# Feed-forward starts on unnormalised rows, and the next layer's modulation dealt out over more places

## What is computed

```python
def trunk_layer(l, x, cond, ctx):
    mod = (silu(cond) @ w_mod[l] + b_mod[l]).reshape(cond.shape[0], 6, D_MODEL)[:, :, None, :]
    h = rmsnorm(x, g_norm1[l]) * (1.0 + mod[:, 1]) + mod[:, 0]
    out, ctx_tensors = token_mixer(l, h, ctx)
    x = x + mod[:, 2] * out
    h = rmsnorm(x, g_norm2[l]) * (1.0 + mod[:, 4]) + mod[:, 3]
    x = x + mod[:, 5] * swiglu(h, w_ffn_in[l], w_ffn_out[l])
    return x, ctx_tensors

def swiglu(h, w_in, w_out):
    gte, up = jnp.split(h @ w_in, 2, axis=-1)
    return (jax.nn.silu(gte) * up) @ w_out
```

## Time and profile before

| | us |
|---|---|
| median of 3 runs | 3496.08 (3495.28 to 3497.89) |
| the profiled execution | 3492.04 |
| its span, first to last instruction | 3490.3 |
| PE busy, PE weight load busy | 3296.3, 3038.3 |
| DVE, ACT, POOL busy | 1967.6, 1114.6, 64.8 |
| mean granted TensorE clock | 0.977 of full |

### The profile page before, as it was taken

One profiled execution on the slowest core, in us unless ns is written; L12 is line 12 of the kernel. 1 busy time (PEld: TensorE's weight loads), 2 busy tenths in 40 slices (PEclk: granted clock), 3 DMA queues, 4 the chain that ended last, 5 costly groups with the idle time before them and its releaser, 6 DMA issues.

```text
span 3490.3 us, 54266 instructions
## 1 busy us (share of the span) xinstructions
PE 3296.3 (94%) x20704; PEld 3038.3 (87%) x20704; DVE 1967.6 (56%) x3034; ACT 1114.6 (32%) x1789; POOL 64.8 (2%) x48
## 2 busy tenths in 40 slices
PE   6899999999998999899999988999999987999999
PEld 3777688999996776899999956899999887999999
DVE  4233357757366665585763745686663788633333
ACT  2244432111134555321111434331111486311111
POOL 0211000000000000000000000000000000000000
PEclk8999999999999999999999999999999999999999
DMA  5111125444221110253532200153532221222222
GB/s 189 55 53 40 39 73 169 140 149 139 77 80 43 44 42 17 61 169 114 175 111 72 70 26 18 55 172 112 173 116 69 76 60 48 67 72 73 77 72 78
DMA packets 443966, 304.23 MB, mean 87 GB/s; under 512 B 12483, under 2 KB 422726, under 8 KB 442822
## 3 DMA queue, kind: packets, MB, share of 16 engines
q1 hardware_dynamic: 433508, 293.75, 27.0%
q10 hardware_dynamic: 10338, 8.88, 0.8%
HBM read 298.49 MB, written 4.10 MB: 87 GB/s over the span
## 4 chain that ended last, share of the span: by engine, by line
PE 85%; DVE 8%; ACT 3%; DVEq 2%; issue 2%; DMA 1%; ACTq 0%; SPq 0%
PE psB L319 30%; PE psA L319 29%; PE psD L319 7%; PE psC L382 3%; PE psA L363 3%; PE psC L335 2%; PE psB L363 2%; PE psC L374 2%; DVE work L2313 1%; PE psD L865 1%; DVE h_lo L2320 1%; DVE act_lo L2320 1%; PE psA L924 1%; DVE work L2627 1%; DMA tables<-in_w_mod 1%
## 5 line engine op out<-in xcount | busy, mean ns | idle before, releaser
L1621 ACT ACTIVATE w_hi<-raw 128x1024 fp32r<-128x1024 f32 (+1 forms) x315 | 325.9, 1036 | 1117.9 <-PE psB L319 758.4
L2215 DVE TENSOR_TENSOR w_lo<-raw,w_hi 128x1024 fp32r<-128x1024 f32 (+1 forms) x315 | 375.2, 1192 | 289.5 <-ACT w_hi L1621 289.1
L319 PE MATMUL psA<-act_hi,w_hi 128*128 128x320 f32 x1600 | 370.5, 313 | 20.4 <-DVE w_lo L2215 15.4
L319 PE MATMUL psB<-act_hi,w_hi 128*128 128x320 f32 x1600 | 369.3, 312 | 10.7 <-DVE w_lo L2215 10.7
L319 PE MATMUL psB<-act_hi,w_lo 128*128 128x320 f32 x1600 | 371.7, 314 | 0.0
L319 PE MATMUL psA<-act_hi,w_lo 128*128 128x320 f32 x1600 | 370.4, 313 | 0.0
L319 PE MATMUL psB<-act_lo,w_hi 128*128 128x320 f32 x1600 | 367.9, 311 | 0.0
L319 PE MATMUL psA<-act_lo,w_hi 128*128 128x320 f32 x1600 | 366.9, 311 | 0.0
L2245 DVE SCALAR_TENSOR_TENSOR work<-work,silu_c 128x1024 f32<-128x1024 f32 x252 | 312.6, 1282 | 11.6
L319 PEld LDWEIGHTS psA<-act_hi,w_hi 128*128 128x128 f32 x1600 | 272.4, 191 | 23.5 <-issue 16.4
L319 PEld LDWEIGHTS psB<-act_hi,w_hi 128*128 128x128 f32 x1600 | 274.8, 191 | 11.4 <-issue 11.4
(11 more groups left out here) (364 smaller groups left out, 5435.5 us busy)
## 6 DMA issues: line engine op xcount, KB each, us to landing
raw<-in_w_ffn_in SPq DMA_DIRECT2D x176, 512.0 KB, 3.8
work<-in_w_mod SPq DMA_DIRECT2D x144, 512.0 KB, 6.0
raw<-in_w_ffn_out SPq DMA_DIRECT2D x64, 512.0 KB, 4.0
raw<-in_w_ffn_out SPq DMA_DIRECT2D x32, 384.0 KB, 3.3
raw<-in_diff_w_in SPq DMA_DIRECT2D x24, 512.0 KB, 3.8
work<-in_w_mod SPq DMA_DIRECT2D x8, 1024.0 KB, 7.2
raw<-in_w_mod SPq DMA_DIRECT2D x16, 512.0 KB, 4.0
tables<-in_w_mod SPq DMA_DIRECT2D x16, 512.0 KB, 4.2
```

The costliest lines, as they stand in the source:

```text
L319: last = nc.tensor.matmul(out[:, b, 0:half], w[slot][:, kt * cols + c0:kt * cols + c0 + P], r[:, o:o + half], start=(kt == 0 and p == 0), ...
L1621: nc.scalar.activation(w_hi[s][:, 0:n], raw[s][:, 0:n], ACT.Copy).then_inc(hi_done, 1)
L2215: nc.vector.tensor_tensor(w_lo[s_][:, 0:n], raw[s_][:, 0:n], w_hi[s_][:, 0:n].bitcast(F32), ALU.subtract).then_inc(split_done, 1)
```

## The change

- **Feed-forward starts** (layers 0 to 3): four panels on unnormalised rows instead of two, that is tiles 0 and 1 with gate and up; tile 2 is the first on normalised rows. DVE rescales panel 1 and splits panel 3 inside the loop of `norm`, and rescales panels 2 and 3 behind it.
- **Layer 1's attention start**: three panels instead of two (query, key, value of head 0). The sums and rotations of head 0 are hung between matmuls of these panels, and four eighths of head 1's query panel go ahead of head 0's scores.
- **Modulation**: units are dealt out by a list of shares over hidden tiles and output turns; `mod_turn` stands at the start of the second place after the one that completes a kind. Kind 5 of layer 0 is dealt out with them as the first kind of its list (7 kinds, 56 units), and `late_wide` and `late_turn` go. Layer 0: 2 2 2 2 3 3 in `in0`, 2 in each turn of `out0`, 3 in each tile of `in1`, 2 in each turn of `out1`, 2 in the first tile of `in2`. Layers 1 and 2: 2 in each tile of `in0` and each turn of `out0`, 3 in each tile of `in1`, 1 in each turn of `out1`. SP issues units four ahead. DVE's loops over output turns are written out in layers 0 to 2.
- **First normalisation**: DVE multiplies x by `first_rms` as soon as that is there; gain and shift then go in two ACT instructions for each tile, in place, ACT copies the tile to hi, and DVE subtracts once for each tile.
- `gains_of` of the next layer stands ahead of the last output projection instead of ahead of chunk 2.

```diff
-FIRST_PANELS = [0, 2, 2, 2, 4, 2, 2, 2]
+MLEAD = 4
+FIRST_PANELS = [0, 4, 3, 4, 4, 4, 2, 4]
...
+        shares = ([2, 2, 2, 2, 3, 3] + [2] * 4 + [3] * 8 + [2] * 4 + [2]) if layer == 0 else [2] * 6 + [2] * 4 + [3] * 8 + [1] * 4
...
                 for g, (place, turn) in enumerate(turns):
+                    turn(place[2])
+                    if g == 2:
+                        mod_units(plan, range(MLEAD))
+                    if g > 2:
+                        mod_units(plan, plan.share(turns[g - 1][0]), MLEAD)
...
-                first_panels(2 * layer + 1, [(psA, 0, ph.number(0, 0)), (psB, 1, ph.number(0, 1))])
-                if layer == 0:
-                    late_wide()
+                first_panels(2 * layer + 1, [(psum[j], j, ph.number(i, j)) for i in range(2) for j in range(2)])
...
-                    first_panels(2, [(psD, 2, phases["diff"].first + 1), (psA, 0, phases["diff"].first + 2)])
-                    ssq(h0)
-                    gv(h0, 0, 2)
-                    acts.wait(pe, "rsq", h0)
-                    rotq(h0)
-                    gv(h0, 2, 4)
-                    ssk(h0)
-                    gv(h0, 4, 6)
+                    first_panels(2, [(psD, 2, first + 1), (psA, 0, first + 2), (psB, 1, first + 3)],
+                                 {(1, 5): lambda: ssq(h0), (2, 1): lambda: rotq(h0), (2, 5): lambda: ssk(h0)})
+                    gq(h1, 0, 2)
                     acts.wait(pe, "rsk", h0)
                     rotk(h0)
-                    gv(h0, 6, 8)
+                    gq(h1, 2, 4)
                     kturn(h0)
...
+                            nc.scalar.activation(source[:, o], source[:, o], ACT.Identity, bias=bias,
+                                                 scale=gains[:, cond * KT + kt:cond * KT + kt + 1])
+                    if n == 0:
+                        act.drain()
+                        last = nc.scalar.activation(hi[:, kt * T:(kt + 1) * T], source[:, kt * T:(kt + 1) * T], ACT.Copy)
...
+            dve.wait_ge(rstd_done, 1)
+            for kt in range(KT):
+                nc.vector.tensor_tensor(first_scaled[:, kt * T:(kt + 1) * T], x[:, kt * T:(kt + 1) * T], first_rms,
+                                        ALU.mult).then_inc(scaled_done, 1)
...
                 norm(n, {1: lambda: rescale(n, 0, psA, ph.number(0, 0), gate_silu),
-                         3: lambda: low_part(f"in{layer}.0", 1, 0)})
-                rescale(n, 1, psB, ph.number(0, 1), prod)
...
+                         3: lambda: low_part(f"in{layer}.0", 1, 0),
+                         5: lambda: rescale(n, 1, psB, ph.number(0, 1), prod),
+                         7: lambda: low_part(f"in{layer}.0", 1, 1)})
...
+                early_product(0, prod, gate_silu)
+                rescale(n, 2, psA, ph.number(1, 0), gate_silu2)
+                low_part(f"in{layer}.0", 2, 0)
+                rescale(n, 3, psB, ph.number(1, 1), prod2)
+                early_hidden(0, prod)
+                low_part(f"in{layer}.0", 2, 1)
+                early_product(1, prod2, gate_silu2)
+                early_hidden(1, prod2)
```

More of the change, by code:

```diff
@@ L121, in number, with __init__, share, plan_modulation @@
         return turn * self.n + (self.first + j + 1)
+class Modulation:
+    def __init__(self, layer, kinds, shares, first_unit, first_kind):
+        self.layer, self.kinds, self.first_unit, self.first_kind = layer, kinds, first_unit, first_kind
+        self.places = [(phase, ch, i) for ch, size in enumerate(FFN_CHUNKS)
+                       for phase, n in (("in", size), ("out", KT // 2)) for i in range(2 if (phase, ch) == ("in", 0) else 0, n)]
+        self.units, self.turns, self.sums = {}, {}, {}
+        at, done = 0, []
+        for p, (place, share) in enumerate(zip(self.places, shares)):
+            self.units[place] = range(at, at + share)
+            if at // KT < (at + share) // KT:
+                done.append(p)
+            at += share
+        assert at == len(kinds) * KT and len(done) == len(kinds)
+        for k, p in enumerate(done):
+            self.turns[self.places[p + 2]] = self.sums[self.places[p + 2]] = k
+            assert k + 2 >= len(kinds) or sum(shares[:p + 3]) <= (k + 2) * KT
+    def share(self, place):
+        return self.units.get(place, range(0))
+def plan_modulation():
+    plans, unit, kind = [], 0, 0
+    for layer in range(DEPTH - 1):
+        kinds = ([(0, 5)] if layer == 0 else []) + [(layer + 1, k) for k in range(6)]
+        shares = ([2, 2, 2, 2, 3, 3] + [2] * 4 + [3] * 8 + [2] * 4 + [2]) if layer == 0 else [2] * 6 + [2] * 4 + [3] * 8 + [1] * 4
+        plans.append(Modulation(layer, kinds, shares, unit, kind))
+        unit, kind = unit + len(kinds) * KT, kind + len(kinds)
+    return plans
 def plan_panels():
@@ L633, in turn, with panels @@
                                      source(g, j)).then_inc(raw_in[s], 16)
-                if units:
-                    turn(0)
-                    for g in range(ph.turns):
-                        if g + 1 < ph.turns:
-                            turn(g + 1)
-                        if behind_first and g == 0:
-                            behind_first()
-                        for u in range(TILE_UNITS):
-                            mod_unit(*units, g * TILE_UNITS + u)
-                    return
+                return turn
+            def panels(name, source):
+                ph, turn = phases[name], panel_turn(name, source)
                 peeled = 1 if ph.first == 0 else 0
@@ L2257, in mod_sums, with place_sums @@
                 last.then_inc(mod_summed, 1)
+                if layer == plan.layer:
+                    dve.drain()
+                    for cond in range(2):
+                        nc.vector.tensor_tensor(m_[:, :, cond], m_[:, :, cond],
+                                                bmod[:, layer * 48 + kind * KT:layer * 48 + (kind + 1) * KT], ALU.add)
+                    dve.drain()
+            def place_sums(plan, place):
+                if plan and place in plan.sums:
+                    mod_sums(plan, plan.sums[place])
             def mod_bias(layer):
                 m = mods[layer % 2][:, :].rearrange("p (k c) -> p k c", c=2)
-                dve.wait_ge(mod_summed, 6 * layer + 1)
+                dve.wait_ge(mod_summed, modulation[layer - 1].first_kind + len(modulation[layer - 1].kinds) + 1)
                 for cond in range(2):
@@ L2528, in _ @@
                     first = phases["diff"].first
-                    norm(2, {1: lambda: rescale(2, 0, psD, first + 1, dq_t[0])})
-                    rescale(2, 1, psA, first + 2, dk_t[0][:, 0:T])
                     h0 = Head(0, 0)
-                    for step in (q_normed, q_roped, k_normed, k_roped):
-                        step(h0)
-                    low(Head(0, 1), 0)
+                    norm(2, {1: lambda: rescale(2, 0, psD, first + 1, dq_t[0]), 3: lambda: low(Head(0, 1), 0),
+                             4: lambda: rescale(2, 1, psA, first + 2, dk_t[0][:, 0:T]), 5: lambda: q_normed(h0),
+                             6: lambda: q_roped(h0), 8: lambda: k_normed(h0)})
+                    rescale(2, 2, psB, first + 3, dvt)
+                    k_roped(h0)
                     low(Head(0, 1), 1)
```

275 lines of the change are left out of this document (128 added, 147 removed).

## The result

| | before | after |
|---|---|---|
| median of the timed executions, us | 3496.98 (3495.28 to 3498.16, 4) | 3440.08 (3439.37 to 3445.85, 4) |
| the profiled execution | 3492.04 | 3440.55 |
| its span | 3490.3 | 3438.8 |
| mean granted clock | 0.977 | 0.980 |

The ratio of after to before is 0.9842, 95% interval 0.9828 to 0.9855: 57 us faster by the medians, 51.5 by the two profiles. Brackets hold the lowest and highest time and, in the table, the number of executions. The forecast was 60.6 us and 3435.4.

What follows compares the result with a forecast made beforehand. PE, busy 94% of the span, was taken as the bound. Savings of 20.9 + 21.9 + 9.8 + 8.0 = 60.6 us took the profiled 3492.04 to 3431.4; plus 4.04 for the median, 3435.4 us, range 3424 to 3459.

Steps and rivals of the forecast that it cites:

- Feed-forward starts: Layers 1 to 3: each start costs 30.5 us, with one 0.96 us wait ahead of panel four and full clock.
- The term of 20.9: Saving in us at the feed-forward starts of layers 1 to 3 together: 7.4, 6.3 and 7.2.
- Layer 0: Its feed-forward start falls from 54.15 to 30.5 us; less 1.74 for one more `mod_turn`, 21.9 us saved.
- Units between output panels at no cost: Output turns: low part, unit and adds take DVE 4.92 us against a panel's 7.11, so cost 0.
- The rival that ends slower: Output turns of layers 0 to 2: late units make PE wait in each of 24, total 3512; chance 0.03.
- the cost of the turns: Layer 0: one `mod_turn` more on PE in plain view, two halves of 0.87, 1.74 us.
- First normalisation: Start of layer 0: ACT paces tiles at 1.87 us, first attention panel ends at 79.5, 9.8 us saved.
- the rule that it cites: Skill rule for the first normalisation: use VectorE, not ScalarE, for adds and multiplications; forecast went by the trace rows instead.
- a like order: First normalisation: old DVE loop with early scaling out of SP's way would end about 1.1 us sooner, sum 61.7.
- Layer 1's attention start: Head 0's scores come 4.3 us earlier, plus about 3.7 from work behind them: 8.0 us saved, bounds 2 and 9.4.
- the second term: Layer 1's attention start, behind head 0's first scores: about 3.7 of the 5.1 us of query panel come out.

Runs made afterwards that it cites:

- old_diff_start: The changed kernel with layer 1's attention start of the kernel before (two panels on unnormalised rows): 3449.47 us, ratio 0.9864.
- both halves: Changed kernel, repeated turn out, fourth panel's low part at step 6 of `norm`, ACT rounding tile 2's gate panel ahead of tile 1's SiLU: 3430.15 us, ratio 0.9802.
- low_part_at_6: Changed kernel with the repeated turn out and DVE's low part of the fourth panel at step 6 of `norm` instead of 7: 3440.02 us, ratio 0.9837.

## Why the forecast came out as it did

It was right in its result (3435.4 against 3440.1, range 3424 to 3459) and in most of its steps, taken one by one:

- **Feed-forward starts: right.** 30.5 us forecast, 30.7 to 30.9 measured, one wait of 0.90 (forecast 0.96), clock 1.00. The term of 20.9 came as 7.4, 6.2 and 6.8, 20.4 without the repeated turns. What was mis-read is small: the forecast had tile 2's low part ready 0.1 ahead of PE, at no cost. It came as counted (1471.20, where PE's rows would have gone on at 1471.28), but PE began 0.25 behind it, and that low part, not the 0.90 ahead of it, was what ended the start.
- **Layer 0: right.** 21.9 forecast, 22.1 measured.
- **Units between output panels at no cost: right,** and with twice the units in a turn still right. The rival that ends slower was not near.
- **The step that failed: the cost of the turns.** It was counted as one `mod_turn` more, in layer 0. The loop helper also makes one turn twice in layers 1 and 2, 3.5 us with no use, on a PE without idle time. It stands in the whole diff and in the order of PE's instructions (32 transposes in a row), and the forecast read neither there.
- **First normalisation: right in size by a wrong route.** 1.87 a tile forecast, 1.90 measured. The forecast for the panel's end, 79.5, was missed by 2.4 (81.9). 1.1 of it is a later start of the tile loop (63.7, not 62.6), as the small matmuls ahead took 6.07 us and not 3.92. Another 1.1 is the panel's last eighth: forecast 0.89, it took 1.97 at a clock of 0.54, and 1.15 at 1.00 in `old_diff_start`:

```profile
79.93:81.90 1.97, 1.97 (x8) 1.97 (x9) 1.41 (x10) 1.25 (x1) 0.00 (x0) 0.54 0.34 83
```

```profile
80.10:81.25 1.15, 1.15 (x8) 1.15 (x9) 0.83 (x6) 1.15 (x1) 0.00 (x0) 1.00 0.13 28
```

The old code has slow cases of the same kind, so over all profiles the difference came out as 9.7 (forecast 9.8), and as 8.0 at the feed-forward start. That ACT's loop was even with DVE's was right, and it hid the better edit: scaling early and giving gain and shift alone to DVE, in two instructions a tile. The forecast, by the rule that it cites, had put 1.1 us on a like order; from the gains to the panel's end it brought 4.8 (13.4 for 18.2).
- **Layer 1's attention start: the mechanism right in its first half, the second term mis-sized.** Scores 4.3 us earlier forecast, 4.5 measured (3.0 in three of the ten profiles of the new code). From the 5.1 us of query panel taken out behind them 3.7 were expected, and some 0.7 came. Stretches from the first scores to the second group of turned probabilities, before:

```profile
1070.97:1085.73 14.76, 12.68 (x58) 9.87 (x59) 7.70 (x17) 4.96 (x12) 0.00 (x0) 0.77 0.32 90
```

and after:

```profile
1039.17:1053.24 14.07, 10.60 (x35) 6.65 (x35) 7.38 (x17) 4.86 (x12) 0.00 (x0) 0.56 0.20 58
```

PE has 23 matmuls less and needs nearly as long. The chain of waits says where the 5.1 us went: pieces on other engines rose from 2.1 to 4.8 us, all of it on ACT (exponentials 0.9 to 1.8, and the value copies with their DMA issues, 1.6, which had been hidden), and PE's own pieces, without the query panel, from 7.5 to 9.3. The clock is 0.56 against 0.77. That the idle time causes the lower clock is likely by the earlier trace rows, but only argued here.

By the parts' means the change saved 8.0 + 22.1 + 5.3 + 5.7 + 4.5 + 6.8 = 52.4 us (4.5 is layer 2's feed-forward part alone, 486.86 to 482.36). The shortfall from 60.6 is the turns (3.5), the attention start (2.7), the first normalisation (1.8) and 0.2 in the rest. The medians stand 57 apart. Where the other 4 us are isn't settled: the profiles of before, at 3492.04 and 3495.77, are both below its median, and the timed executions have no profile. The medians of the undone first normalisation and attention start likewise lie 4 to 6 us above what their parts say.

## What to carry to other kernels

Add up PE's own work in a stage that doesn't run at PE's pace, since that sum (29.53 us here) is both the bound of any reordering and the mark that tells when it is reached. Before a small wait is taken away, look at what is ready next on the other engines: the first half of that edit gained nothing, since the next low part was as late, and both halves gained more than the wait's length. A handover without a listed wait can still be the one that sets the end. Compare stages and not totals, and only after a second profile of the same code has told which of them repeat.

## What the runs showed of the hardware

- Waits of PE of 0.90 us (changed kernel) and 1.14 us (`low_part_at_6`, layer 1) left the granted clock at 1.00. Behind one of 2.09 us, in layer 3 of the latter, it was 0.57 over the next 3.6 us.
- PE began tile 2 0.24 or 0.25 us after its low part was done, once with a wait of 1.14 us in the profile's list and once with none.
- The same small matmuls behind the same wait of 2.0 us took 3.92 to 6.86 us in fourteen profiles. In the shortest case the clock was 1.00 up to 60 us and 0.85 from there to their end; in the changed kernel (6.07) it was 0.64 from 57 to 60 us and 0.50 behind. The Trainium skill (TensorE: Matmul & The Clock Gate, Part 1) says that the point of change differs between runs of one kernel; these profiles agree.
- Gain and shift from two columns, 128 and 512 elements: 1.18 us on ACT, 0.81 on DVE.
- One load of 512 KB took 14.11 us where the median is 3.8; it cost PE 2.1 us of waiting and a slow panel (8.89 us).
